# Gates and projections of three branches laid into a sparse attention, and two small moves at the start

## Chip, cores, metric

One core of a Trainium2 chip. The time is that of the device, from the kernel's start to its end, in microseconds (us), as the median of several runs. The profile is of one further execution.

## What is computed

One decoder layer for 512 prompt tokens and 8 sample tokens (each with 2048 cached), all float32, width 1024. The part that matters:

```
h = rms_norm(x, n1);  z = h @ w_in                    # 39 chunks of 128 columns
o_gla, o_hgrn (chunked linear attentions), o_pool (trailing means), o_nsa (sparse attention)
proj = einsum('blnc,ncd->blnd', branches, w_branch)   # 4 x (512 -> 1024)
gate = sigmoid(h @ w_gate + b_gate)                   # 4 x (1024 -> 1024)
x = x + sum_n(gate * proj) @ w_out
u = relu(rms_norm(x, n2) @ w1);  x = x + (u * u) @ w2
fgate = lb + (1 - lb) * sigmoid(hf)                   # lb: from the cumulated softmax of a parameter
```

The sparse attention adds three branches: mean-compressed keys, the 16 best blocks of 64 keys, and a window of 512. For the prompt it is a dense masked attention over up to four blocks of 128 keys; for the samples it reads the caches.

## The kernel before

All 520 tokens are the columns of one stage; activations lie with features on partitions (eight tiles of 128 x 520). A float32 product is made of three fp32r ones: `hi x hi`, `lo x hi`, `hi x lo`. So every weight chunk (128 partitions x 1024, 512 KB) is loaded by SyncE (`load`, `reload`, slots of a ring of four), rounded to its high part by ScalarE (`upper`, L1048) and subtracted for its low part by GpSimd (`lower`, L1876, the operation at L1879). A unit is one chunk times all tokens: `fm_unit` (L545, the matmuls at L555), 48 matmuls of 260 columns into two banks of PSUM. `UNITS_OF` counts the units of each chunk; the semaphores `raw`, `w_hi`, `w_lo` and `prod` chain the four engines. The order on each engine is that in which its block is written.

The stages, in the profiled execution:

- 0 to 50 us: transposes of x, first norm (`norm_apply`, L1303), h in two parts.
- to 437: the 39 chunks of `w_in`, laid between the steps of the two linear attentions, their norms and the pooling. The lower bound's exp is at L1092 (ScalarE), its four small VectorE steps at L1351 to L1354, and TensorE's L616 waits for the VectorE work behind them (`la_ev`, L1357). GpSimd makes the distances of seven levels (L1890, L1891), with low parts between.
- 437 to 509, preparation: norms of the keys, compressed keys of the prompt, masks and small tables. GpSimd gathers the compressed cache of one sample after the other (2 MB each, L1946) into two buffers `Y`, and sums 16 rows to one (L1964, L1965).
- 509 to 657, pair loop: 32 pairs of heads; eight pairs each for one, two, three and four blocks of keys. Each pair: scores (L888), mask and maximum (L1703, L1705), exp (L1219), transposes (L861), copies (L1714), values (L874). The samples' compressed attention and choice of blocks run as single operations between the pairs (`compressed_step`).
- 657 to 736, sample jobs: ten jobs, first two for the window (`Y`, loaded by SyncE), then eight of the chosen cache, each of four slices of 512 KB, gathered by GpSimd (L1980) into a ring `X` of 15. A job: `keys_transposed` (L924), `scores` (L934), `probs_over` (L945), `values` (L955). Its partial sums are merged at L1761 to L1781.
- 736 to 767: x is read back from a spill, h is made again (its place was used by the attention), by `norm_apply`.
- 767 to 1041, mixing: for each of 8 tiles of 128 output columns four gates and four projections: 48 chunks, 64 units. Sigmoid on ScalarE, products and sums on VectorE (`mixT`).
- to 1502: `w_out` with the second norm's sums, the MLP, transposes, output.

## Time and profile before

| | us |
|---|---|
| runs (3): median, lowest, highest | 1506.16, 1505.02, 1507.02 |
| profiled execution, its time | 1503.8 |
| its span, first to last instruction | 1502.0 |
| TensorE busy | 1298.2 |
| VectorE, ScalarE, GpSimd busy | 568.0, 403.9, 542.9 |

The span is what the engines' instructions cover; the time has what lies around it too. A group's mean is the duration of one instruction; TensorE's overlap, so that their rate is the stretch divided by their number. "Idle before" is put down to what released the engine last.

### The profile page before, as it was taken

How to read it: one execution, taken by the hardware profiler on the slowest of the kernel's cores; microseconds unless marked ns; L12 is line 12 of the kernel's file. 1: busy time of each engine (PE TensorE's matmuls, PEld its weight loads, DVE VectorE, ACT ScalarE, POOL GpSimd, SP SyncE). 2: the span in 40 equal slices, each digit the busy share in tenths (PEclk: the TensorE clock that was granted, in tenths of full speed). 3: DMA queues.
4: the chain of work that ended last, by engine and by line, in shares of the span. 5: the costliest groups of instructions: out<-in, count | busy, mean ns of one | idle time of the engine just before them, and what ended most of it. 6: DMA issues, size and time to landing. Idle time of an engine off the chain costs nothing.

```text
span 1502.0 us, 24320 instructions
## 1 busy us (share of the span) xinstructions
PE 1298.2 (86%) x10284; PEld 1220.6 (81%) x10284; DVE 568.0 (38%) x800; ACT 403.9 (27%) x605; POOL 542.9 (36%) x262
## 2 busy tenths in 40 slices
PE   4698998998974477786489999997979999999998
PEld 3598997897863355565389999997969999999998
DVE  3433664261435776764571111112133410134102
ACT  3342212013450123222152322233232211122210
POOL 2335432054129900025033434343324434344341
PEclk9799999999985698898679999999989999999999
DMA  4221001532145510038113232322212322323222
GB/s 160 99 72 56 29 29 57 125 104 79 32 174 218 208 73 1 1 117 332 57 43 99 84 98 84 98 85 83 71 50 91 93 90 85 94 87 96 86 86 83
DMA packets 43585, 139.15 MB, mean 93 GB/s; under 512 B 3975, under 2 KB 15595, under 8 KB 42107
## 3 DMA queue, kind: packets, MB, share of 16 engines
q1 hardware_dynamic: 37762, 104.70, 21.9%
q0 software_dynamic: 5760, 33.56, 6.1%
q8 instruction: 48, 0.79, 0.2%
q14 instruction: 15, 0.11, 0.0%
HBM read 129.97 MB, written 8.49 MB: 92 GB/s over the span
## 4 chain that ended last, share of the span: by engine, by line
PE 76%; DVE 13%; issue 3%; DMA 3%; ACT 2%; POOL 1%; DVEq 0%; ACTq 0%
PE PS L555 53%; PE PS L583 7%; PE PS L635 3%; DVE tmp L1309 2%; DMA M<-cache_slc_kv,idx 2%; PE PS L874 1%; PE PS L888 1%; PE PS L924 1%; DMA M<-weights 1%; DVE hL L1313 1%; DVE M L1714 1%; PE PS L861 1%; PE PS L773 1%; PE PS L726 1%; PE PS L670 1%
## 5 line engine op out<-in xcount | busy, mean ns | idle before, releaser
L1879 POOL TENSOR_TENSOR WL<-M,WH 128x1024 fp32r<-128x1024 f32 x159 | 386.7, 2435 | 693.3 <-ACT WH L1051 693.1
L555 PE MATMUL PS<-hH,WH 128*128 128x260 f32 x1424 | 298.1, 291 | 30.3 <-DVE hL L1313 27.4
L1051 ACT CAST WH<-M 128x1024 fp32r<-128x1024 f32 x159 | 166.2, 1049 | 505.0 <-DMA M<-weights 505.0
L555 PE MATMUL PS<-hL,WH 128*128 128x260 f32 x1424 | 293.2, 288 | 0.0
L555 PE MATMUL PS<-hH,WL 128*128 128x260 f32 x1424 | 292.9, 288 | 0.0
L555 PEld LDWEIGHTS PS<-hH,WH 128*128 128x128 f32 x1424 | 226.2, 194 | 36.6 <-DVE hL L1313 14.0
L555 PEld LDWEIGHTS PS<-hL,WH 128*128 128x128 f32 x1424 | 226.2, 194 | 0.0
L555 PEld LDWEIGHTS PS<-hH,WL 128*128 128x128 f32 x1424 | 226.1, 194 | 0.0
L555 PE MATMUL PS<-uH,WH 128*128 128x260 f32 x512 | 103.2, 283 | 2.4 <-ACT M L1291 2.4
L555 PE MATMUL PS<-uH,WL 128*128 128x260 f32 x512 | 103.2, 283 | 0.0
L555 PE MATMUL PS<-uL,WH 128*128 128x260 f32 x512 | 103.0, 283 | 0.0
L1980 POOL DMA_INDIRECT M<-cache_slc_kv,idx x32 | 30.1, 941 | 163.0 <-DVE M L1727 127.5
L583 PE MATMUL PS<-WH,hH 128*128 128x256 f32 (+1 forms) x280 | 83.9, 300 | 5.2 <-POOL WL L1879 4.3
L555 PEld LDWEIGHTS PS<-uH,WH 128*128 128x128 f32 x512 | 78.9, 188 | 2.8 <-issue 2.8
L583 PE MATMUL PS<-WL,hH 128*128 128x256 f32 (+1 forms) x280 | 79.5, 284 | 0.0
L583 PE MATMUL PS<-WH,hL 128*128 128x256 f32 (+1 forms) x280 | 79.3, 283 | 0.0
L555 PEld LDWEIGHTS PS<-uH,WL 128*128 128x128 f32 x512 | 78.9, 188 | 0.0
L555 PEld LDWEIGHTS PS<-uL,WH 128*128 128x128 f32 x512 | 78.7, 188 | 0.0
L1852 DVE TENSOR_TENSOR tmp<-M 128x520 f32<-128x520 f32 x32 | 38.2, 1192 | 103.8 <-ACT M L1291 103.8
L1862 DVE TENSOR_TENSOR xT<-xT,PS 128x520 f32 x16 | 11.1, 697 | 171.3 <-PE PS L555 171.3
L1964 POOL TENSOR_TENSOR M<-M 128x2048 f32<-128x2048 f32 (+2 forms) x24 | 66.2, 2759 | 7.9 <-DMA M<-cache_cmp_kv,idx 6.6
L1219 ACT ACTIVATE M<-PS,stat 128x128 f32<-128x128 f32 (+3 forms) x64 | 33.2, 523 | 126.7 <-DVE stat L1705 126.7
(347 smaller groups left out, 2008.8 us busy)
## 6 DMA issues: line engine op xcount, KB each, us to landing
M<-weights SPq DMA_DIRECT2D x159, 512.0 KB, 3.5
M<-cache_win_kv SPq DMA_DIRECT2D x2, 2048.0 KB, 7.9
spill<-xT SPq DMA_DIRECT2D x1, 2080.0 KB, 10.2
xT<-spill SPq DMA_DIRECT2D x1, 2080.0 KB, 8.8
M<-x_prompt SPq DMA_DIRECT2D x4, 512.0 KB
y_prompt<-M SPq DMA_DIRECT2D x4, 512.0 KB
con<-tables SPq DMA_DIRECT2D x1, 1437.5 KB, 12.4
M<-state_gla SPq DMA_DIRECT2D x2, 512.0 KB, 6.1
```

What stands on the lines that cost most here:

```text
L555: last = mm(PS[:, bank + h, 0:HALF], w[:, n % 4, k, :], x[:, HALF * h:HALF * h + HALF], start=(start and k == k0 and w is WH and x is hi), ...
L583: last = mm(PS[0:m, bank, 0:pieces * cols], x[:, k, t], w[:, n % 4:n % 4 + pieces, k, 0:cols], start=(k == 0 and x is hH and w is WH), sto ...
L635: last = mm(PS[:, g % 4, 128 * k:128 * k + 128], a, a, start=True, stop=True)
L670: last = mm(o, zt[:, c, head_cols(k, par)[0]], SC[:, 2 * c + par, k], start=True, stop=(c == 0))
L726: last = mm(PS[:, 2 * (e % 2) + h, 0:HALF], ones if kind == "o" else BO, SQ[e % 2][:, HALF * h:HALF * h + HALF], start=True, stop=True)
L1051: nc.scalar.copy(WH[:, n % 4].rearrange("p k n -> p (k n)"), WR[:, n % 4]).then_inc(sem("w_hi"), 1)
L1219: f(P[2 * (p % 2) + c][:, 0:128 * i + 128], PS[:, 2 * (p % 2) + c, 0:128 * i + 128], ACT.Exp, bias=nm[p % 2][:, c:c + 1], accum_out=rs[:, ...
L1309: v.scalar_tensor_tensor(TH[k % 2], xT[:, k], V(g, k, k + 1), RST, ALU.mult, ALU.mult)\
L1852: v.tensor_tensor(US[q % 2], UR[q % 2], UR[q % 2], ALU.mult).then_inc(sem("u_sq"), 1)
L1879: p.tensor_tensor(WL[:, n % 4].rearrange("p k n -> p (k n)"), WR[:, n % 4], WH[:, n % 4].rearrange("p k n -> p (k n)"), ALU.subtract).then ...
L1964: step(p.tensor_tensor(t[:, 0:n], t[:, 0:n], t[:, n:2 * n], ALU.add))
L1980: gp.indirect_dma_start(X[ring(n)].rearrange("p i c -> p (i c)"), None, slices, bass.IndirectOffsetOnAxis(idx[:, at:at + 1], 0)).then_inc( ...
```

## The change

Three of the four branches (pool, gla, hgrn: `ORDER = (2, 0, 1)`) get their gates and projections before the sparse attention is done. Their 36 chunks come first, in three chunks for every 256 output columns (two of gates, one of projections), and are cut into 96 steps `MIX`: a step is half the tokens of one tile of 128 columns, into one bank. A gate step has 24 matmuls, a projection step 12. 32 steps stand in the preparation, 48 in the pair loop (three in two pairs), 16 in the sample jobs. For that:

- h and the weights keep their places through the attention. Weight slots are three while it runs (`slot_of`, `chunk_behind`); the fourth one's high and low parts are buffers `W3` for the compressed cache.
- The compressed cache comes in quarters of a sample: 32 gathers of 512 KB (`CPIECES`), each summed and added up, between the low parts of the chunks. The samples' compressed operations come four half steps later; `SHIFTS` has their places.
- The ring for the sample jobs has ten slices (`XR`), window slices included, and all are issued by GpSimd. Slices 0 to 9 come early: 0 and 1 in the loop, 2 to 5 when the choice of blocks and step 63 are done, 6 to 9 after the loop.
- Banks: the transposed probabilities have one bank (4) instead of two, bank 7 is that of the steps; the jobs' keys have two banks for their transposes instead of four, which VectorE and ScalarE now empty in turn.
- sigmoid(y) is made as tanh(y / 2) + 1, and the sum is halved where `w_out`'s result is added to x. The branch's own high part is `bX`, one buffer for the three.
- The fourth branch remains behind the attention, in 12 chunks and 16 units, with its high and low parts alone; h isn't made again. Its first gate units stand ahead of the merge's transposes. x is read back to another place, `x2`, after the attention.

Apart from that, the lower bound's subtraction goes to VectorE's start, its exp directly behind the first norm's root, its other steps ahead of the gates' copy; the low parts of chunks 9 and 10 go ahead of the first distances. The core of the diff (TensorE's steps also stand at fixed places in the preparation):

```diff
-N_OUT, N_MLP = N_MIX + 48, N_MIX + 56
-UNITS_OF += [1, 1, 2] * 16 + [1] * 72
+N_LAST, N_OUT, N_MLP = N_MIX + 36, N_MIX + 48, N_MIX + 56
+UNITS_OF += [2, 2, 4] * 12 + [1, 1, 2] * 4 + [1] * 72
 NCH = len(UNITS_OF)
+
+
+def slot_of(n):
+
+    return n % 4 if n < N_MIX else n % 3 if n < N_LAST else (n - N_LAST) % 4
+
+
...
+def chunk_behind(n):
+
+    if n < N_MIX or n > N_LAST + 3:
+        return n - 4
+    return n - 3
+
+
+ORDER = (2, 0, 1)
+MIX = []
+for _bi in range(3):
+    for _m in range(4):
+        for _s in range(8):
+            _t = _s // 2 % 2
+            MIX.append((_bi, _m, _t, _s % 2, _s < 4, N_MIX + 12 * _bi + 3 * _m + (_t if _s < 4 else 2)))
...
+PREP, LOOP = 32, 48
+
+
+def mix_bank(k):
+
+    return 7 if PREP <= k < PREP + LOOP else 6 + k % 2
+
+
+def mix_evac(k):
+
+    bi, m, t, h, gate, _ = MIX[k]
+    return ("sg" if gate else "mix_mul"), 16 * bi + 4 * m + 2 * t + h + 1
 
...
-        Y = [R[:, 12416 + 4096 * i:12416 + 4096 * (i + 1)] for i in range(2)]
...
-        X = [R[:, a:a + 1024].rearrange("p (i c) -> p i c", i=4)
-             for a in [7168 + 1024 * i for i in range(5)] + [12416 + 1024 * i for i in range(8)] + [5120, 6144]]
-        AGAIN = list(range(9)) + [13, 14]
...
+        W3 = [R[:, 12416 + 3072:12416 + 4096], R[:, 16512 + 3072:16512 + 4096]]
+        CPIECES = [(x, c) for x in (4, 5, 6, 7, 0, 1, 2, 3) for c in range(4)]
+        SHIFTS = {24: 4, 26: 6, 32: 0, 34: 2}
+        XR = W3 + [zu[:, 0:1024], zu[:, 1024:2048], zg[:, 0:1024], zg[:, 1024:2048]]             + [zt[:, i, CQ:CQ + 1024] for i in range(4)]
...
+            def mix_step(k):
+
+                bi, m, t, h, gate, n = MIX[k]
+                if h == 0 and (gate or t == 0):
+                    pe.wait_ge(sem("w_lo"), n + 1)
+                earlier = [e for e in range(k) if mix_bank(e) == mix_bank(k)]
+                if earlier:
+                    pe.wait_ge(sem(mix_evac(earlier[-1])[0]), mix_evac(earlier[-1])[1])
+                if not gate and t + h == 0 and m == 0:
+                    pe.wait_ge(sem("b_lo"), bi + 1)
+                half = slice(HALF * h, HALF * h + HALF)
+                for c in range(KT if gate else 4):
+                    hi, lo = hk(c) if gate else (bX[:, c], bL[ORDER[bi]][:, c])
+                    at = c if gate else 4 * t + c
+                    for w, x in ((WH, hi), (WH, lo), (WL, hi)):
+                        last = mm(PS[:, mix_bank(k), 0:HALF], w[:, slot_of(n), at, :], x[:, half],
+                                  start=(c == 0 and w is WH and x is hi), stop=(c == (KT if gate else 4) - 1 and w is WL))
+                last.then_inc(sem("prod"), 1)
+
+            def mix_steps(a, b):
+
+                for k in range(a, b):
+                    mix_step(k)
+
...
+                    if p < NP and 3 * p // 2 + c < 3 * (p + 1) // 2:
+                        mix_step(PREP + 3 * p // 2 + c)
...
             def keys_transposed(j):
 
-                b, y, c = JOBS[j]
-                if b:
-                    pe.wait_ge(sem(f"xw{y}"), 16)
-                else:
-                    pe.wait_ge(sem(f"xq{(j - 2) % 4}"), 64 * ((j - 2) // 4 + 1))
+                pe.wait_ge(sem(f"xq{j % 3}"), 64 * (j // 3 + 1))
                 for s in range(4):
-                    if j:
-                        pe.wait_ge(sem(("kx_dve", "kx_act")[s // 2]), 2 * j - 1 + s % 2)
+                    if s >= 2:
+                        pe.wait_ge(sem(("kx_dve", "kx_act")[s % 2]), 2 * j + 1)
+                    elif j:
+                        pe.wait_ge(sem(("kx_dve", "kx_act")[s % 2]), 2 * j)
                     for i in range(4):
-                        last = tr(PS[:, s, 128 * i:128 * i + 128], piece(j, s, i)[0], ident)
+                        last = tr(PS[:, s % 2, 128 * i:128 * i + 128], piece(j, s, i)[0], ident)
                     last.then_inc(sem("ks_mm"), 1)
...
+                    if j < 6:
+                        mix_step(PREP + LOOP + 2 * j + 2)
...
+            act.wait_ge(*done("lb_d"))
+            f(lbv[:, :, 1], lbv[:, :, 0], ACT.Exp).then_inc(once("lb_e"), 1)
...
+            def mix_step(k):
+
+                bi, m, t, h, gate, n = MIX[k]
+                half = slice(HALF * h, HALF * h + HALF)
+                if gate:
+                    act.wait_ge(sem("prod"), units_before(N_MIX) + k + 1)
+                    if bi + m:
+                        act.wait_ge(sem("mix_mul"), 16 * bi + 4 * m - 4 + 2 * t + h + 1)
+                    col = 8 * ORDER[bi] + 2 * m + t
+                    f(SG[t][:, half], PS[:, mix_bank(k), 0:HALF], ACT.Tanh, bias=bgh[:, col:col + 1], scale=0.5)\
+                        .then_inc(sem("sg"), 1)
+                    if m + t == 0 and h == 1:
+                        if bi:
+                            act.wait_ge(sem("prod"), units_before(N_MIX) + 32 * bi)
+                        else:
+                            act.wait_ge(sem("pool_ev"), 4)
+                            act.wait_ge(sem("stored"), 48)
+                        b = ORDER[bi]
+                        nc.scalar.copy(bX, zf[:, 4 * b:4 * b + 4]).then_inc(sem("b_hi"), 1)
+                s = 4 * (not gate) + 2 * t + h
+                if s in (2, 4, 6):
+                    upper(N_MIX + 12 * bi + 3 * m + 1 + s // 2)
+
+            act.wait_ge(sem("st_out"), 128)
...
+                    dve.wait_ge(sem("sg"), u)
+                    if bi > 1 or bi and u > 18:
+                        dve.wait_ge(sem("mix_add"), u - 16 - 2)
+                    out = GP[:, half] if bi else mixT[:, 2 * m + t, half]
+                    v.scalar_tensor_tensor(out, SG[t][:, half], 1.0, PS[:, mix_bank(k), 0:HALF], ALU.add, ALU.mult)\
+                        .then_inc(sem("mix_mul"), 1)
+                    if bi:
+                        dve.wait_ge(sem("mix_mul"), u)
+                        v.tensor_tensor(mixT[:, 2 * m + t, half], mixT[:, 2 * m + t, half], GP[:, half], ALU.add)\
+                            .then_inc(sem("mix_add"), 1)
...
-            norm_apply("n3", "n1")
-            for b in range(4):
-                dve.wait_ge(sem("b_hi"), b + 1)
-                v.tensor_tensor(bL[b], zf[:, 4 * b:4 * b + 4], bH[b], ALU.subtract).then_inc(sem("b_lo"), 1)
-            with dve.Fori(0, 4) as dq:
...
-            for n in range(9):
+            for n in range(11):
                 lower(n)
             gp.wait_ge(sem("cum"), 4)
             distances(0)
-            lower(9)
-            lower(10)
             distances(1)
             for n in (11, 12, 13):
...
+            rows = lambda name: A[name].rearrange("o n (r t) a k d -> (o n r) (t a k d)", t=4)
+
+            def compressed_gather(q):
+
+                if q >= 2:
+                    gp.wait_ge(sem("c_red"), q - 1)
+                x, c = CPIECES[q]
+                gp.indirect_dma_start(W3[q % 2], None, rows("cache_cmp_kv"),
+                                      bass.IndirectOffsetOnAxis(idx[:, NI + NS * c + x:NI + NS * c + x + 1], 0))\
+                  .then_inc(sem(f"xc{q % 2}"), 16)
+
+            def compressed_sum(q):
+
+                x, c = CPIECES[q]
+                gp.wait_ge(sem(f"xc{q % 2}"), 16 * (q // 2 + 1))
+                t = W3[q % 2].rearrange("p (t c) -> p t c", t=4)
+                step(p.tensor_tensor(t[:, 0:2], t[:, 0:2], t[:, 2:4], ALU.add))
+                if c == 0:
+                    if x == 4:
+                        gp.wait_ge(sem("pool_mm"), 4)
+                    if x == 0:
+                        gp.wait_ge(sem("rows_out"), 96)
+                        gp.wait_ge(*done("ckv_mm"))
+                    p.tensor_tensor(S16[x], t[:, 0], t[:, 1], ALU.add).then_inc(sem("c_red"), 1)
+                else:
+                    step(p.tensor_tensor(t[:, 0], t[:, 0], t[:, 1], ALU.add))
+                    gp.wait_ge(sem("c_red"), q)
+                    p.tensor_tensor(S16[x], S16[x], t[:, 0], ALU.add).then_inc(sem("c_red"), 1)
+                if q + 2 < len(CPIECES):
+                    compressed_gather(q + 2)
+
             gp.wait_ge(*done("idx"))
-            gp.wait_ge(sem("prod"), units_before(N_MIX))
-            for x in range(NS + 1):
-                if x < NS:
-                    if x >= 2:
-                        gp.wait_ge(sem("c_red"), x - 1)
-                    gather(Y[x % 2], x, "cache_cmp_kv").then_inc(sem(f"xc{x % 2}"), 16)
-                if x:
-
-                    y = x - 1
-                    gp.wait_ge(sem(f"xc{y % 2}"), 16 * (y // 2 + 1))
-                    if y == 0:
-                        gp.wait_ge(sem("pool_mm"), 4)
-                        gp.wait_ge(sem("stored"), 48)
-                    t = Y[y % 2].rearrange("p (t c) -> p t c", t=16)
-                    for n in (8, 4, 2):
-                        step(p.tensor_tensor(t[:, 0:n], t[:, 0:n], t[:, n:2 * n], ALU.add))
-                    p.tensor_tensor(S16[y], t[:, 0], t[:, 1], ALU.add).then_inc(sem("c_red"), 1)
-
-            gp.wait_ge(sem("on"), 2 * TT)
-            slices = A["cache_slc_kv"].rearrange("o n (r t) a k d -> (o n r) (t a k d)", t=4)
-            for n in range(32):
+            gp.wait_ge(sem("prod"), units_to_free(N_MIX - 4))
+            compressed_gather(0)
+            compressed_gather(1)
+            lower(N_MIX)
+            lower(N_MIX + 1)
+            q = 0
+            for n in range(N_MIX + 2, N_MIX + 22):
+                for _ in range((2, 1, 1)[n % 3] if n < N_MIX + 12 else 3):
+                    if q < len(CPIECES):
+                        compressed_sum(q)
+                        q += 1
+                lower(n)
+
+            def cache_piece(n):
+
+
                 j, s = n // 4, n % 4
-                y, c = JOBS[2 + j][1:3]
-                if 5 <= n < 13:
-                    gp.wait_ge(sem("oq_mm"), 1 + (n - 5) // 4)
-                if n == 13:
-                    gp.wait_ge(sem("ont_mm"), TT)
-                if n >= 15:
-                    before = AGAIN[n - 15] if n < 26 else n - 11
-                    gp.wait_ge(sem("oq_mm"), 3 + before // 4)
-                at = NI + NS + 4 * (4 * y + s) + c
-                gp.indirect_dma_start(X[ring(n)].rearrange("p i c -> p (i c)"), None, slices,
-                                      bass.IndirectOffsetOnAxis(idx[:, at:at + 1], 0)).then_inc(sem(f"xq{j % 4}"), 16)
-            gp.wait_ge(sem("oq_mm"), NJ)
-            with gp.Fori(0, 30) as i:
+                b, y, c = JOBS[j]
+                if n == 0:
+                    gp.wait_ge(sem("c_red"), len(CPIECES))
+                if n == 2:
+                    gp.wait_ge(*done("rank"))
+                if n == 4:
+                    gp.wait_ge(sem("prod"), units_before(N_MIX) + 64)
+                if n == 6:
+                    gp.wait_ge(sem("on"), 2 * TT)
+                if n >= 10 and n % 4 == 2:
+                    gp.wait_ge(sem("oq_mm"), (n - 10) // 4 + 1)
+                x = 4 * y + s
+                if b:
+                    src = A["cache_win_kv"].rearrange("o s (p i) a k d -> p (o s) (i a k d)", i=4)[:, x]
+                    gp.dma_start(XR[n % 10], src).then_inc(sem(f"xq{j % 3}"), 16)
+                else:
+                    at = NI + 4 * NS + 4 * x + c
+                    gp.indirect_dma_start(XR[n % 10], None, rows("cache_slc_kv"),
+                                          bass.IndirectOffsetOnAxis(idx[:, at:at + 1], 0)).then_inc(sem(f"xq{j % 3}"), 16)
+
+            for n in range(2):
+                cache_piece(n)
+            for n in range(N_MIX + 22, N_MIX + 31):
+                lower(n)
+            for n in range(2, 10):
+                cache_piece(n)
+            for n in range(10, 4 * NJ):
+                if n % 4 == 2 and N_MIX + 31 + n // 4 - 2 < N_LAST:
```

## Rows read from the trace of the kernel before

**Rows 1.** The page, parts 1 and 2: share of TensorE, its clock in 40 slices.
```profile
PE 1298.2 (86%) x10284; PEld 1220.6 (81%) x10284; DVE 568.0 (38%) x800; ACT 403.9 (27%) x605; POOL 542.9 (36%) x262
...
PEclk9799999999985698898679999999989999999999
```

**Rows 2.** Busy time by stretch: us, each engine's busy us (instructions), clock, DMA.
```profile
437.00:509.00 72.00, 27.32 (x110) 22.12 (x109) 45.24 (x54) 9.07 (x12) 61.05 (x30) 0.59 0.62 227
509.00:657.00 148.00, 114.82 (x688) 87.18 (x689) 104.78 (x197) 39.52 (x134) 19.73 (x11) 0.84 0.12 43
657.00:736.00 79.00, 54.46 (x620) 42.33 (x622) 35.81 (x55) 20.21 (x49) 30.05 (x32) 0.83 0.66 240
736.00:767.00 31.00, 10.89 (x52) 9.11 (x45) 27.40 (x51) 10.20 (x18) 10.11 (x4) 0.57 0.00 1
767.00:1041.00 274.00, 274.00 (x2267) 274.00 (x2266) 53.93 (x59) 83.36 (x87) 111.38 (x47) 0.99 0.28 90
1041.00:1049.00 8.00, 0.37 (x4) 0.16 (x2) 3.92 (x3) 3.95 (x7) 3.91 (x2) 0.71 0.25 67
```

**Rows 3.** Waits of TensorE, 40 to 440 us: total, times, longest.
```profile
PE PS L616 <- DVE M L1357: 9.5, 1, 9.5
...
PE PS L583 <- POOL WL L1879: 4.3, 1, 4.3
```

**Rows 4.** Timeline of GpSimd, 100 to 130 us: start, us, line, operation.
```profile
106.13 1.90 POOL L1890 TENSOR_TENSOR M<-M 128x1024 f32<-128x1024 f32 x1 [10.80 <-DVE M L1380]
...
109.83 5.73 POOL L1879 TENSOR_TENSOR WL<-M,WH 128x1024 fp32r<-128x1024 f32 x2
```

**Rows 5.** Chain that ended last, 14 to 135 us: start, us, what.
```profile
74.90 13.34 PE PS L555 x96
```

**Rows 6.** Groups of GpSimd by form: count, busy us, mean ns, idle before.
```profile
L1879 POOL TENSOR_TENSOR WL<-M,WH 128x1024 fp32r<-128x1024 f32 x159 | 386.7, 2435 | 693.3 <-ACT WH L1051 693.1
...
L1964 POOL TENSOR_TENSOR M<-M 128x512 f32<-128x512 f32 x8 | 10.4, 1305 | 0.6
...
L1946 POOL DMA_INDIRECT M<-cache_cmp_kv,idx x8 | 7.9, 987 | 20.4 <-PE PS L555 18.5 <-POOL M L1965 1.6 <-issue 0.3
...
L1965 POOL TENSOR_TENSOR M<-M 128x256 f32<-128x256 f32 x8 | 6.7, 834 | 0.6
```

**Rows 7.** The slice gathers' line L1980, to landing.
```profile
DMA to landing us min/median/max: 4.1/5.9/8.7
```

**Rows 8.** Timeline of ScalarE, 430 to 450 us.
```profile
442.59 0.22 ACT L1194 ACTIVATE stat<-stat 128x20 f32<-128x20 f32 x1
```

**Rows 9.** The page, part 6: transfers, issue to landing.
```profile
M<-weights SPq DMA_DIRECT2D x159, 512.0 KB, 3.5
```

**Rows 10.** Timeline of the pair loop, 509 to 657 us.
```profile
520.79 3.81 DVE L1721 TENSOR_TENSOR stat<-stat,M 128x8 f32<-128x8 f32 x1
...
603.55 1.95 PE L831 MATMUL PS<-gaT,M 127*128 127x8 f32 x16 [0.95 <-DVE gaT L1656]
...
646.82 1.13 PE L888 MATMUL PS<-M 64*128 64x512 f32 x4
...
650.59 0.62 PE L861 MATMUL PS<-con,M 128*128 128x128 f32 x4
```

**Rows 11.** Timeline of the sample jobs, 657 to 737 us.
```profile
659.96 1.97 PE L924 MATMUL PS<-con,M 128*128 128x128 f32 x16 [0.18 <-DVE M L1730]
...
725.84 3.68 PE L924 MATMUL PS<-con,M 128*128 128x128 f32 x16 [4.52 <-DMA M<-cache_slc_kv,idx]
...
731.21 1.05 PE L955 MATMUL PS<-M 128*32 128x128 f32 x32
...
735.22 1.08 PE L955 MATMUL PS<-M 128*32 128x128 f32 x32 [0.78 <-DVE M L1795]
```

**Rows 12.** Timeline behind the jobs.
```profile
749.06 0.78 DVE L1808 COPY M<-M 64x16 f32<-64x16 f32 x4
```

**Rows 13.** Timeline of ScalarE in the loop: a table load.
```profile
565.48 1.28 ACT L1205 ACT_TABLE_LOAD   x1
```

More of the change, by code:

```diff
@@ L169, in build @@
         bL = [parts(f"bL{b}", 4 * b * T, 4) for b in range(4)]
-        bH = [parts(f"bH{b}", (16 + 4 * b) * T, 4) for b in range(4)]
-        mL, mH = parts("mL", 32 * T, KT), parts("mH", 16 * T, KT)
+        bX = place("bX", 20 * T, 4 * TM).rearrange("p (i c) -> p i c", c=TM)[:, :, 0:T]
+        bH3 = parts("bH3", ZU * T, 4)
+        mL, mH = parts("mL", 24 * T, KT), parts("mH", 16 * T, KT)
         uH, uL = parts("uH", 0, 16), parts("uL", 16 * T, 16)
@@ L490, in _ @@
                          tail[HIST:HIST + NS]).then_inc(sem("stored"), 16)
-            sp.wait_ge(sem("pd"), 8)
-            sp.dma_start(SPARE, A["spill"]).then_inc(sem("xt_back"), 16)
+            for n in range(N_MIX, N_MIX + 3):
+                reload(n)
             sp.wait_ge(*done("k_norm"))
@@ L974, in _ @@
+            last_gate(0, 1)
             pe.wait_ge(*done("nsa_done"))
[L975 to L989 removed]
@@ L2017 @@
     gate = tiles(a["w_gate"][0]).reshape(4, 8, 128, KT, COLS)
-    branch = [tiles(a["w_branch"][0].reshape(2, 1024, 1024)[i]) for i in range(2)]
-    mix = np.stack([gate[0], gate[1], branch[0], gate[2], gate[3], branch[1]], 1).reshape(48, 128, KT, COLS)
+    branch = [a["w_branch"][0, b].reshape(4, 128, 4, 2, COLS).transpose(2, 1, 3, 0, 4).reshape(4, 128, KT, COLS)
+              for b in range(4)]
+    mix = np.concatenate([np.stack([gate[b, 0::2], gate[b, 1::2], branch[b]], 1).reshape(12, 128, KT, COLS)
+                          for b in (2, 0, 1, 3)])
     w1, w2 = a["mlp_w1"][0], a["mlp_w2"][0]
```

579 lines of the change are left out of this document (326 added, 253 removed).

## The prediction

> **What bounds the kernel now.** I read the page first: TensorE is busy for 86% of the span, and its granted clock dips in one stretch, slices 12 to 20 [rows 1]. The table of stretches shows why [rows 2]. From 767 to 1041 us, the gates and projections of all four branches, 2267 matmuls run in 274 us: 0.121 us each, nothing idle, clock 0.99. From 437 to 767 us, the sparse attention, TensorE issues few instructions, its clock is 0.57 to 0.84, and it waits for VectorE, ScalarE and DMAs in turn. So matmul work of the first kind, put into the holes of the second, is what can be gained. Three quarters of it move: 96 steps, of which 48 gate steps have 24 matmuls (2.90 us) and 48 projection steps 12 (1.45 us), together 209 us. The question is how much the stretches grow when these are laid in. I take the four stages in order, each as growth against the profiled execution.
>
> **Start (to 135 us).** TensorE waits 9.5 us for the gate's VectorE work, and 4.3 us for a low part on GpSimd [rows 3]. The first wait is the lower bound: VectorE waited in its queue for ScalarE's exp of two columns, which stood behind a weight cast and two activations. With exp right after the norm, and its VectorE steps ahead of the gates' copy, nothing of that is left; next in line is a weight chunk that had landed. The second: chunks 9 and 10 (5.73 us on GpSimd) stand between the first two rounds of distances, after the sums that end at 106.1 [rows 4]. They now run ahead of those sums, so chunk 11 comes about 5 us earlier after them. The matmuls behind the first wait began at the lower clock (96 in 13.34 us [rows 5], where 0.121 each would be 11.6), and I assume the same behind the second: 3 us more. The added index operations are six of 128 x 8 or so, beside matmuls already queued. Behind this comes a stretch that is pure TensorE. Total 9.5 + 4.3 + 3: **-17 us** (bounds -8, if the sigmoid chain takes the place, and -20).
>
> **Preparation and pair loop (437 to 657).** The new owner is GpSimd. The cache sums were 8 rounds; now each quarter is gathered by itself: 32 rounds. A round is one addition over 512 elements (1.31), one over 256 and, for three of four, another to accumulate (0.73 to 0.83), a gather (0.99) and some 0.3 of issue: 3.35 or 4.1, mean **3.95 us**; each low part is 2.44 [rows 6]. The order is fixed: 13 rounds and 12 low parts before the 32 preparation steps can end, then three rounds before each of the next six low parts. A gather has two rounds' time less its own additions to land; at 5.9 us [rows 7] that is (5.9 + 3.0) / 2 = 4.45 a round, under which the low parts between fit. Chunk 40 is cast behind the roots of the keys' norms: those end at 442.8 now [rows 8], and get the compressed keys' root with two table loads, some 3 us, and two casts ahead of them, so about 448. From there 13 x 3.95 + 11 x 2.44 + some 5 of first waits = 83 us bring chunk 50 at 532, TensorE's last step at 538. The loop starts at 509 now [rows 2], so preparation grows 29 us for 70 us of matmuls. Weights aren't the limit: 3.5 us from issue to landing [rows 9], against a chunk's 5.8 us of matmuls with two other slots full.
>
> Then 19 rounds and 7 low parts, 92 us: chunk 57 comes at **624**, and pair 11 waits for it. TensorE alone would need some 60 us here; the difference is lost to GpSimd. From pair 11 TensorE is the bound. Its own part of a four-block pair is the distance from scores to the end of the second head: 646.82 to 650.59, 3.8 us [rows 10]; for three and two blocks I scale to 2.7 and 1.9. Each pair gets 1.5 steps, 3.26 us, and I add 0.4 for handovers: 5.6, 6.4 and 7.5 us. 5 x 5.6 + 8 x 6.4 + 8 x 7.5 = 139, the compressed branch's own matmuls 12 (an estimate: six groups like the one of 1.95 us [rows 10]), the last pairs and sums 4: end at **779** against 656.7. Growth **122 us**, with 174 us of matmuls in it (bounds 96, GpSimd hidden, and 165). The score banks are left with one transpose bank less; the copy it waits for (0.7 us) lies under a step, or costs 0.5 where there is one step only.
>
> The rule that speaks against this is the lock. In the trace an 8-column VectorE multiply took 3.81 us at 520.79 [rows 10], while GpSimd was summing the cache. The Trainium skill, "SBUF — State Buffer", section "SBUF: two separate sides", says that a VectorE operation with two SBUF inputs blocks for the whole GpSimd instruction; by it each of the 24 accumulations in the loop could wait up to a low part, which the trace bears out. 24 x 2.44 = 59 us is its upper end; half of a low part each, 29 us, is its price as a rival. In the sum I take it as covered, since VectorE is busy for 105 us of the loop's 148 [rows 2] and the loop gets 122 - 29 = 93 us longer for 24 products and 24 accumulations of 260 columns.
>
> **Sample jobs (657 to 736).** Here I expect a loss. The ring was 15 slices and two window buffers; it is ten, and slices 10 and 11, the second half of job 2, may be gathered only when job 0's values are through. TensorE goes from values(j) straight to the keys of job j + 2, so from job 2 each job waits: 0.3 + 1.25 (second issue) + 5.2 (between 4.1 and 5.9 [rows 7]) = 6.75 us. The 16 steps stand after the first half of the keys and ahead of the values, that is, not under this wait; they push the release back. A job from landed keys to values, 725.84 to 732.3, is 6.4 us at the low clock: the same 16 transposes take 1.97 us warm and 3.68 after 4.5 us of idling for a DMA [rows 11]. Steps add 26 us over eight jobs (five gates, eight projections), and 0.55 a job because the first one starts cold. Period 6.75 + 6.4 + 3.3 + 0.55 = **17.0**; the first values come 21.4 us after the loop (three steps in it), eight periods 136, last values 2.5: 160 us, against 79.6 now (656.7 to 736.3). Growth **80** (bounds 58, warm with landings of 4.1, and 105).
>
> The Trainium skill, "TensorE: Matmul & The Clock Gate", section "What's actually happening", has two levels, 1.2 and 2.4 GHz; 3.68 over 1.97 is near that ratio, and by the level alone all 26 us of steps would be 52 if every job stayed cold. That is the rival on the far side below.
>
> **After the jobs (736 to 1049).** The norm of h again and its splits (749.8 to 767) go; h is kept. nsa_done comes 13.5 us after the last values (749.84 - 736.3 [rows 11, 12]), one gate unit fills it (5.8 us), the second gate unit 5.8 follows, the branch's cast and low part add 4.6 behind nsa_done, so the projections start at 18.5. Then 10 units of 5.8 us: 76.5, and 2 more to the output's first matmul, as the mix's casts are now spread; before, 8 us passed there [rows 2]. 78.5 against 1049.2 - 736.3 = 313: **-234.5**, of which 209 is moved work (bounds -225, if the 2 MB of x2 ahead of chunk 79 bites, and -238). Sigmoid as tanh + 1, halved in the output's addition, replaces one operation by one.
>
> **Sum.** -17 + 122 + 80 - 234.5 = -49.5 on 1503.8 us: 1454.3. The median of the runs is 2.4 above the profiled time, so **1457 us**.
>
> **Rivals.**
> 1. *Jobs better, loop as said*: landings near 4.1 and a warm engine; 8 x 2.6 = 21 less: **1436**. For: a lone gather lands in 4.1. Against: after a wait the transposes ran cold.
> 2. *VectorE's lock becomes the loop's bound*: +29: **1486**. For: 3.81 us for 8 columns; against: VectorE's slack.
> 3. *Rounds cost more*: if gathers compete with weights and rows, a round becomes 4.65: 32 x 0.7 = +22: **1479**.
> 4. *Tanh and exp reload tables.* A change of function cost 1.28 us at 565.48 [rows 13]; two loads for each of 24 gate steps in the loop, half exposed, and 8 later: +35: **1492**. No row shows tanh. (The Trainium skill, "ScalarE: Activation LUTs", section "Table sets: the hidden batching unit", puts both in one set: then nothing.)
> 5. *Slower*: in the jobs the wait keeps TensorE cold throughout. Place: jobs 2 to 9. Price: period 6.75 + 7.1 + 6.6 = 20.4, and with landings at 8.7 [rows 7] 24: 8 x 7 = +56: **1513**. It decides from a period of 23.2 us. For: the clock is 0.83 already, with a wait in only some of the jobs [rows 2]; against: steps are dense work.
> 6. That the steps hide fully, everywhere: under 1424.
>
> **How the numbers follow.** Forecast 0.42 (own range 1443 to 1472); rivals 1 to 6: 0.17, 0.13, 0.09, 0.05, 0.10, 0.04. The range reaches from 1424 to 1494. This kernel's measurement tells 0.2%, 3 us, from nothing. Slower: 0.08 of rival 5 and 0.02 from the tails of 2 and 4; same 0.03; faster 0.87.
>
> **What would show it.** Right: chunk 57's low part near 610 (less 17 for the start), TensorE idle before it; pairs of 7.5 us at the end; job periods of 17 us with a DMA wait near 6 in each; no wait of 9.5 near 65. Wrong: idle TensorE in the late loop (rival 2), table loads beside tanh (4), no DMA wait in the jobs (1), a period over 23 (5).

## The result, and the profile after

| | us | ratio to before, 95% interval |
|---|---|---|
| before, measured beside it (4 runs) | 1506.59 | |
| after (4 runs) | 1530.35, from 1529.07 to 1531.31 | 1.0159, 1.0141 to 1.0176 |
| forecast | 1457, range 1424 to 1494 | |

The change made the kernel 1.6% slower where I forecast 3.3% faster, and the time lies outside my range. TensorE's instructions are as many as before and its share of the longer span is the same 86%. From the page, parts 1 and 2, of the kernel after, beside [rows 1]:

```profile
PE 1310.4 (86%) x10284; PEld 1230.4 (81%) x10284; DVE 573.4 (38%) x823; ACT 394.2 (26%) x615; POOL 587.0 (38%) x350
...
PEclk9899999999987888899997978799989999999999
```

The low clock didn't go: its lowest tenths rose from 5 to 7, over a longer middle. Busy time by stretch of the kernel after (columns as in [rows 2]): preparation, the pairs that GpSimd holds, the late pairs, the sample jobs, the merge, the last branch.

```profile
436.00:541.00 105.00, 86.49 (x578) 83.97 (x577) 37.94 (x54) 21.85 (x30) 72.42 (x58) 0.81 0.38 122
541.00:633.00 92.00, 58.79 (x401) 53.97 (x399) 26.93 (x50) 20.78 (x55) 81.39 (x74) 0.83 0.47 148
648.00:816.00 168.00, 149.00 (x1045) 125.90 (x1044) 98.34 (x159) 48.08 (x114) 31.87 (x17) 0.92 0.14 47
833.00:993.00 160.00, 98.26 (x858) 85.00 (x862) 40.27 (x67) 29.70 (x60) 47.71 (x41) 0.79 0.38 132
993.00:1012.00 19.00, 8.76 (x115) 7.82 (x105) 13.91 (x35) 4.57 (x11) 4.64 (x2) 0.89 0.08 28
1012.00:1077.00 65.00, 65.00 (x534) 65.00 (x534) 24.46 (x27) 21.37 (x26) 24.40 (x10) 0.98 0.35 123
```

The ledger, from the first instruction of each stage in the two traces (the jobs to the end of their last values, at 736.3 and 997.7; `w_out` begins at 1049.2 and 1076.5):

| stage | forecast | measured | off |
|---|---|---|---|
| start, at the last unit of `w_in` (431.61 to 422.26) | -17 | -9.4 | +7.6 |
| preparation and pair loop (end 656.7 to 832.8, less the start) | +122 | +185.5 | +63.5 |
| jobs (79.6 to 164.9) | +80 | +85.3 | +5.3 |
| last values to `w_out` (312.9 to 78.8) | -234.5 | -234.1 | +0.4 |
| sum | -49.5 | +27.3 | +76.8 |

The spans differ by 25.1 (1502.0 to 1527.1); some 2 us are regained behind `w_out`'s first matmul. So one term holds most of the miss, and it has two halves. The forecast had chunk 57's low part done at 624, or 614.6 with the real start: it was done at 638.7, 24.1 late. From there to the end of the loop I gave 155 us: it took 194.1, 39.1 more.

The first half, GpSimd's low parts and the casts that they waited for. From its timeline: start, us, operation, and in brackets the idle time before it. The low parts shown are those of chunks 44, 47, 50 and 57.

```profile
490.58 2.36 POOL L2045 TENSOR_TENSOR WL<-M,WH 128x1024 fp32r<-128x1024 f32 x1 [13.91 <-ACT WH L1138]
...
518.01 2.40 POOL L2045 TENSOR_TENSOR WL<-M,WH 128x1024 fp32r<-128x1024 f32 x1 [4.68 <-ACT WH L1138]
...
544.10 2.36 POOL L2045 TENSOR_TENSOR WL<-M,WH 128x1024 fp32r<-128x1024 f32 x1 [3.28 <-ACT WH L1138]
...
636.08 2.57 POOL L2045 TENSOR_TENSOR WL<-M,WH 128x1024 fp32r<-128x1024 f32 x1
```

And ScalarE's timeline in front of chunk 44's cast: the exponent of the prompt's compressed scores, then the tanh of two steps, then the cast.

```profile
483.95 1.06 ACT L1316 ACTIVATE M<-M 128x1024 f32<-128x1024 f32 x1 [11.06 <-DVE M L1719]
486.20 0.48 ACT L1286 ACTIVATE tmp<-PS,stat 128x260 f32<-128x260 f32 x1 [1.19 <-PE PS L790]
489.08 0.48 ACT L1286 ACTIVATE tmp<-PS,stat 128x260 f32<-128x260 f32 x1 [2.41 <-PE PS L790]
489.46 1.04 ACT L1138 CAST WH<-M 128x1024 fp32r<-128x1024 f32 x1
```

GpSimd stood 13.9 us at this one low part, with 27 rounds of the compressed cache behind it in its queue that needed nothing from ScalarE. With chunk 41's 4.6 the waits are 26.5 us, and the low part of chunk 40, where they begin to count, was itself done at 442.7, 4 us behind the forecast (448, less the start's 9.4). The rounds themselves went as forecast: 92.2 us from the end of chunk 50's low part (546.5) to that of chunk 57's, where 92 were said.

The second half. Maxima of pairs 11 and 31 before, then after (timelines of VectorE):

```profile
540.19 0.69 DVE L1705 TENSOR_REDUCE stat<-PS 128x2 f32<-128x512 f32 x1
...
648.46 1.23 DVE L1705 TENSOR_REDUCE stat<-PS 128x2 f32<-128x1024 f32 x1
```

```profile
647.72 0.69 DVE L1863 TENSOR_REDUCE stat<-PS 128x2 f32<-128x512 f32 x1
...
816.20 1.23 DVE L1863 TENSOR_REDUCE stat<-PS 128x2 f32<-128x1024 f32 x1
```

These 20 pairs took 108.3 us before and take 168.5 now. Busy time of that stretch before, and of the steps' matmuls alone in the one after:

```profile
540.00:648.50 108.50, 86.71 (x515) 64.64 (x514) 75.18 (x134) 28.55 (x86) 0.00 (x0) 0.87 0.00 1
```

```profile
648.00:816.00 168.00, 75.70 (x549) 70.27 (x547) 0.92 0.14 47
```

TensorE was busy for 80% of these pairs before, 21.8 us idle in 108.5. The steps bring 75.7 us, the stretch grows by 60, and 19.0 us are still idle. So the steps found next to no holes: the idle time fell by 2.8 us. The other 13 us between 75.7 and 60 are TensorE's busy time outside the steps, 73.3 us (149.0 - 75.7) where it was 86.7. Not all of that is faster work. Records of neighbouring matmuls overlap, and a moment in which both a step and a pair are busy counts among the steps; the pairs' values, transposes and scores, each line for itself, take 78.9 us where they took 83.2.

The jobs did what the forecast said. TensorE between two jobs' values in the kernel after (the steps' own lines left out):

```profile
898.06 1.97 PE L987 MATMUL PS<-con,M 128*128 128x128 f32 x8 [7.00 <-DMA M<-cache_slc_kv,idx]
...
902.28 1.04 PE L987 MATMUL PS<-con,M 128*128 128x128 f32 x8
903.15 0.60 PE L1010 MATMUL PS<-con,M 128*128 128x128 f32 x4
904.04 1.07 PE L999 MATMUL PS<-M 128*32 128x512 f32 x8 [0.29 <-DVE M L1904]
...
908.11 1.08 PE L1020 MATMUL PS<-M 128*32 128x128 f32 x32
```

A wait of 7.0 us here and of 7.2 in the mean of eight, the longest 9.5 (6.75 forecast), first keys cold at 1.97 for 8 (1.04 for the second 8), a mean period of 17.2 us (17.0 forecast). Everything between the keys and the values is covered, and the steps stand there, while the wait behind the values has nothing in it.

### The profile page after: what moved, and what is told of

Read it like the earlier page. It is cut to its first block, busy times and chain, and to the rows that moved or that the text cites. A ratio compares the mean times of both kernels' runs of the same rounds, so it can differ in the third digit from the quotient of the medians.

```text
span 1527.1 us, 24112 instructions
## 1 busy us (share of the span) xinstructions
PE 1310.4 (86%) x10284; PEld 1230.4 (81%) x10284; DVE 573.4 (38%) x823; ACT 394.2 (26%) x615; POOL 587.0 (38%) x350
## 3 DMA queue, kind: packets, MB, share of 16 engines
q1 hardware_dynamic: 36706, 100.50, 20.1%
## 4 chain that ended last, share of the span: by engine, by line
PE 71%; DVE 9%; POOL 9%; DMA 3%; ACT 3%; issue 3%; DVEq 0%; POOLq 0%; ACTq 0%
PE PS L582 38%; PE PS L790 10%; PE PS L610 7%; DMA M<-cache_slc_kv,idx 3%; PE PS L662 3%; POOL WL L2045 2%; POOL M L2125 2%; PE PS L987 2%; POOL M L2116 1%; PE PS L922 1%; PE PS L935 1%; PE PS L951 1%; DVE tmp L1431 1%; POOL M L2134 1%; POOL M L2136 1%
## 5 line engine op out<-in xcount | busy, mean ns | idle before, releaser
L582 PE MATMUL PS<-hH,WH 128*128 128x260 f32 x1040 | 218.1, 292 | 22.2 <-DVE hL L1435 18.8
L582 PE MATMUL PS<-hL,WH 128*128 128x260 f32 x1040 | 213.9, 288 | 0.0
L582 PE MATMUL PS<-hH,WL 128*128 128x260 f32 x1040 | 213.8, 288 | 0.0
L582 PEld LDWEIGHTS PS<-hH,WH 128*128 128x128 f32 x1040 | 165.3, 194 | 27.5 <-issue 11.4
L582 PEld LDWEIGHTS PS<-hL,WH 128*128 128x128 f32 x1040 | 165.2, 194 | 0.0
L582 PEld LDWEIGHTS PS<-hH,WL 128*128 128x128 f32 x1040 | 165.0, 194 | 0.0
L790 PE MATMUL PS<-hH,WH 128*128 128x260 f32 x384 | 124.3, 324 | 36.0 <-POOL WL L2045 35.8
L790 PE MATMUL PS<-hL,WH 128*128 128x260 f32 x384 | 119.1, 310 | 0.0
L790 PE MATMUL PS<-hH,WL 128*128 128x260 f32 x384 | 118.5, 309 | 0.0
L790 PEld LDWEIGHTS PS<-hH,WH 128*128 128x128 f32 x384 | 84.5, 220 | 41.1 <-POOL WL L2045 37.7
L790 PEld LDWEIGHTS PS<-hL,WH 128*128 128x128 f32 x384 | 84.1, 219 | 0.0
L790 PEld LDWEIGHTS PS<-hH,WL 128*128 128x128 f32 x384 | 83.4, 217 | 0.0
L582 PEld LDWEIGHTS PS<-uH,WH 128*128 128x128 f32 x512 | 78.9, 188 | 2.8 <-issue 2.8
L2017 DVE TENSOR_TENSOR tmp<-M 128x520 f32<-128x520 f32 x32 | 42.5, 1329 | 100.0 <-ACT M L1413 100.0
L987 PE MATMUL PS<-con,M 128*128 128x128 f32 x160 | 29.1, 342 | 58.4 <-DMA M<-cache_slc_kv,idx 57.3
```

Of the source, the lines that this page charges most:

```text
L582: last = mm(PS[:, bank + h, 0:HALF], w[:, slot_of(n), k, :], x[:, HALF * h:HALF * h + HALF], start=(start and k == k0 and w is WH and x is ...
L790: last = mm(PS[:, mix_bank(k), 0:HALF], w[:, slot_of(n), at, :], x[:, half], start=(c == 0 and w is WH and x is hi), stop=(c == (KT if gat ...
L987: last = tr(PS[:, s % 2, 128 * i:128 * i + 128], piece(j, s, i)[0], ident)
L2017: v.tensor_tensor(US[q % 2], UR[q % 2], UR[q % 2], ALU.mult).then_inc(sem("u_sq"), 1)
```

## Experiments

My theories after the comparison: GpSimd's fixed order, with the casts it waits for, holds preparation and first pairs; in the jobs the steps stand in the wrong place; the late pairs are set either by VectorE's handovers, one transpose bank among them, or by TensorE's own work.

**1. The start alone**, on the kernel before (the diff is the last hunks of the change: exp and subtraction moved, `range(9)` to `range(11)`).

> The kernel before with the two small moves alone: the lower bound's operations ahead of the matmuls and the low parts of chunks 9 and 10 ahead of the distances. My theory (the moves take away one wait of TensorE and pull the low parts of 11 to 13 forward, as the changed kernel's trace shows, where the last unit of w_in ends 9.4 us earlier): 1497 us, between 1494 and 1500, faster by 0.5 to 0.8%. Rival (the 9.4 us are given back by the time of the pair loop or the jobs, whose transfers and low parts keep their own pace): 1503 to 1507.

1494.02 us, ratio 0.9923 (0.9905 to 0.9940): 11 us where it isn't followed by the rest, against 17 forecast.

**2. The bound's part of it alone**, the low parts of 9 and 10 left behind the first distances.

> The kernel before with the lower bound's operations moved alone; the two low parts stay behind the first distances. My forecast priced the bound's part at 9.5 us and the low parts at 4.3 and 3; both together measured about 11 us. Theory (the bound's wait is the larger part): 1498 to 1503 where both together gave 1494. Rival (the low parts alone gave it): 1503 to 1507.

1495.89 us, 0.9925 (0.9907 to 0.9943): the same ratio, so the times don't show the low parts' share. The bound's move is nearly all. First matmul behind the distances, before its 135.7, here and then with both moves (line, instruction, durations, first and last start):

```profile
L637 PE MATMUL PS<-M x64: 272/272/373, 127.2 to 135.4; 64*128 64x128 f32 x64
```

```profile
L637 PE MATMUL PS<-M x64: 272/272/373, 124.3 to 132.5; 64*128 64x128 f32 x64
```

8.5 us from the bound, 2.9 from the low parts, which I had priced at 4.3 + 3. The wait that I priced didn't go, and nor did the low clock behind it: TensorE still stands at chunk 11's low part, for 4.31 us with the bound's move alone and for 4.14 with both, only 3.4 us earlier, and from 110 to 115 us the granted clock is 0.50 with both. Its wait, with the bound's move alone and then with both:

```profile
PE PS L583 <- POOL WL L1881: 4.3, 1, 4.3
```

```profile
PE PS L583 <- POOL WL L1881: 4.1, 1, 4.1
```

One reason: the sums that the distances wait for now run beside the two low parts that were moved. VectorE's four sums after and before:

```profile
91.41 8.43 DVE L1505 TENSOR_TENSOR_SCAN M<-con,M 128x512 f32<-128x512 f32 x4
```

```profile
101.49 4.56 DVE L1380 TENSOR_TENSOR_SCAN M<-con,M 128x512 f32<-128x512 f32 x4
```

8.43 us for what took 4.56. The two experiments differ alike: 8.43 with both moves, where the longest of the four takes 3.35 us, and 4.56 with the bound's alone, the longest 1.22. The Trainium skill, "SBUF — State Buffer", section "SBUF: two separate sides", has a VectorE operation with two SBUF inputs and a GpSimd operation that reads SBUF wait for each other, the later one for the whole of the earlier; the trace agrees, with 3.9 us lost beside low parts of 2.4 and 2.7 us.

**3. Both steps of a job behind its values**, on the kernel after:

```diff
                     last.then_inc(sem("ks_mm"), 1)
-                    if s == 1:
-                        mix_step(PREP + LOOP + j + min(max(j - 1, 0), 6))
...
                     scores(j + 1)
-                    if j < 6:
-                        mix_step(PREP + LOOP + 2 * j + 2)
                 values(j)
+                if j < 8:
+                    mix_step(PREP + LOOP + 2 * j)
+                    mix_step(PREP + LOOP + 2 * j + 1)
```

(likewise on ScalarE and VectorE; GpSimd's low parts 71 to 74 go behind the first four gathers that a job releases.)

> The changed kernel with both steps of a sample job put right behind the job's values and ahead of the next keys, where TensorE waits about 7 us for the gather (57.3 us in 8 waits). Theory (the wait is a fixed time from the values, about 7 us, so two steps of together 4 to 5.5 us in it are free): the waits fall to about 2 us each, the handovers that the steps covered come back at 0.5 to 1.5 us a job, jobs 160 -> 128 to 138 us, total 1500 to 1508. Rival A (the copies and the exponent behind the keys need the steps' cover as much): jobs 150 us or more, total 1518 to 1530. Rival B (the gathers are late for their own reason and move with the queue): no change, 1527 to 1533.

1496.84 us, 0.9942 (0.9923 to 0.9961), 34 us less than after and better than I expected. Waits for the gathers, total, times, longest (57.3 in 8 before the edit):

```profile
PE PS L987 <- DMA M<-cache_slc_kv,idx: 19.6, 8, 4.9
```

The mean period is 12.65 us instead of 17.2, the whole stage 123.5 instead of 164.9. That is 41 us; 4 of them are lost ahead of the jobs, where nothing was edited: pair 11's maximum stands at 652.0 in this trace, at 647.7 in that of after. The handovers needed no cover worth naming. So the wait was in my forecast, to half a microsecond, and what stood in the wrong place cost more than the whole change was slower by.

**4. The rounds thinned**, on the kernel after: additions of 8 elements instead of 512 and 256 (the sums are left out, so the kernel only serves to read the path).

> The changed kernel with its 32 rounds of the compressed cache thinned: the gathers stay, the three additions of a round are cut to 8 elements a row (their sums are left out, so this time is only for reading the path). Theory (GpSimd, in order, bounds the preparation and the first pairs): a round falls from 4.15 to about 1.9 us, chunk 57's low part comes about 40 us earlier or more, the pair loop ends 30 to 50 us earlier, total 1480 to 1500. Rival (TensorE and VectorE's handover take over at once, since the late pairs cost as much as the early): total 1515 to 1528.

1482.06 us. Chunk 57's low part is done 47 us earlier, at 591.5, the loop ends at 781.8 (51 earlier), and the late part between them takes 190.3 us where it took 194.1. GpSimd bounds the first half and has next to nothing to do with the second.

**5. The casts one step earlier**, the additions whole:

```diff
-                if s in (2, 4, 6):
-                    upper(N_MIX + 12 * bi + 3 * m + 1 + s // 2)
+                if s in (1, 3, 5):
+                    upper(N_MIX + 12 * bi + 3 * m + 1 + (s + 1) // 2)
```

> The changed kernel with ScalarE's casts of the mix chunks one step earlier (behind the first, third and fifth step's place instead of the second, fourth and sixth). Theory (GpSimd stood 4.6, 13.9, 4.7 and 3.3 us at low parts whose cast was not done, with its rounds queued behind them, and the early loop is bound by GpSimd): chunk 50's low part 15 to 25 us earlier, total 1508 to 1518. Rival (casts wait for the weights' transfer, so ScalarE is held instead and its exponents with it): 1528 to 1540.

1508.89 us, 1.0020 (1.0001 to 1.0039): 21 us less than after from two lines, as the theory said. Low parts of chunks 44, 50 and 57 (490.58, 544.10 and 636.08 before the edit):

```profile
479.77 2.39 POOL L2045 TENSOR_TENSOR WL<-M,WH 128x1024 fp32r<-128x1024 f32 x1 [8.80 <-ACT WH L1138]
...
525.40 2.40 POOL L2045 TENSOR_TENSOR WL<-M,WH 128x1024 fp32r<-128x1024 f32 x1
...
616.99 2.35 POOL L2045 TENSOR_TENSOR WL<-M,WH 128x1024 fp32r<-128x1024 f32 x1
```

The late part is 190.3 us, as in experiment 4 and 3.8 less than in the changed kernel. Most of the first half of the miss, 19 of 24 us, is this.

**6. One transpose bank in the kernel before**, `PS[:, (4, 7)[c]` to `PS[:, 4` with the wait for the last copy.

> The kernel before with the transposes of both heads of a pair in one PSUM bank, as the changed kernel has them (its second bank went to the steps). Theory (part of the 39 us that the late pairs cost above my forecast is this handover: a head's transposes now wait until VectorE has copied the other's): the pair loop 8 to 25 us longer, 1513 to 1530. Rival (the loop's matmuls and the exponent hide it, as the waits of only 0.3 to 2.4 us each suggest): 1503 to 1509.

1531.38 us, 1.0160 (1.0143 to 1.0178): the lost bank alone costs the kernel before 23.5 us, its pair loop 25.4. Its maxima of pairs 11 and 31 stand at 548.1 and 672.0: 123.9 us for the 20 pairs, where 108.3 were. TensorE's largest wait from 540 to 672 us, the late pairs:

```profile
PE PS L861 <- DVE M L1714: 21.9, 20, 2.7
```

I had priced that bank at 0.5 us where one step covers it.

**7. The second head's transposes in its own score bank**, on the kernel after:

```diff
-                    last = tr(PS[:, 4, 128 * j:128 * j + 128], P[...
+                bank = 2 * (p % 2) + 1 if c else 4
+                    last = tr(PS[:, bank, 128 * j:128 * j + 128], P[...
...
+                        if p >= 2 and c:
+                            pe.wait_ge(sem("pt_ev"), 2 * p - 2)
```

> The changed kernel with the second head's transposes in that head's own score bank (free once its exponent is taken), so that the two heads of a pair no longer share one bank. Theory (the shared bank cost the kernel before 23.5 us and its pair loop 25.4 us, and the late pairs of the changed kernel are set by such handovers, since cutting the steps' matmuls shortened them by only 28 us of 197): the late stretch 197 -> 175 to 185 us, the loop's start unchanged (GpSimd), total 1508 to 1520. Rival (with steps between the two heads' transposes the copy is covered already, 9.6 us in 8 waits is all there is): 1522 to 1531.

1529.88 us, 1.0145 (1.0126 to 1.0165): no difference that can be told from after. The waits of L922 on VectorE are gone from the late pairs, whose 20 periods fall from 168.5 to 162.5 us, but pair 11 came 5 us later. Experiment 3's trace has its pair 11 as late (652.0), with the shared bank and 168.6 us behind it. The rival was right: with steps between the heads' transposes the copy is covered. What cost 23.5 us in the kernel before costs at most 6 here. Why pair 11 was later in the two traces isn't settled.

**8. The loop's steps thinned** to 3 matmuls each, on the kernel after (their sums are left out, again only to read the path):

> The changed kernel with the 48 steps of the pair loop cut to their first product chunk (3 matmuls each instead of 24 or 12; their sums are left out, so this time is only for reading the path); waits, tanh, products and low parts stay. Theory (from chunk 57 on TensorE's own matmuls are most of the loop, 175.7 us busy in 200, and before it GpSimd is the bound): the stretch from chunk 57's low part to the transposes behind the loop 197 -> 130 to 150 us, the stretch before it unchanged within 10 us, total 1465 to 1485. Rival (VectorE's order sets the late pairs): it stays above 165 us, total 1490 or more.

1507.13 us. The late part falls by 27 us (from 194.1 to 166.9), so my expectation was wrong, and both numbers are where the rival had them: 54.7 us of the steps' busy time were taken out between pairs 11 and 31, and half of that came off. Whole stretch from pair 11 to 31, and the steps' part of it:

```profile
651.00:792.00 141.00, 103.23 (x588) 76.94 (x588) 99.70 (x161) 46.99 (x114) 31.37 (x17) 0.85 0.17 51
```

```profile
651.00:792.00 141.00, 21.00 (x90) 15.01 (x90) 0.85 0.17 51
```

The other half came back in two ways. TensorE's idle time is 38 us instead of 19: with the matmuls cut, the copies that they covered stand free, 19.7 of it waiting for L1873's copies in 17 places (6.9 in 5 before the cut). And its busy time without the steps is 82.2 us at a granted clock of 0.85, against 73.3 (149.0 - 75.7) with full steps at 0.92. Part of these 9 us is again the overlap of records; values, transposes and scores, each line for itself, go from 78.9 to 86.4 us, and the lower clock is what I put that down to. No run changes the clock alone.

So this experiment doesn't decide between TensorE's own work and VectorE's handovers as the bound of the late pairs. The 20 pairs took 123.9 us with one bank and no steps (experiment 6), 141 with the thin steps' 21.0 us and 168.5 with the full ones' 75.7. The first 21 us of steps hid 4 of themselves, the next 54.7 hid 27. I read it so: full steps fill the path and cover waits at once, and the sum of the pairs' own work and the steps' is what holds. That reading is argued from these sums.

**9. Casts earlier, and ten low parts on VectorE** (chunks 41 to 50), GpSimd doing 22 rounds in one go, then 2 before each low part:

```diff
+                if s in (2, 4, 6) and n_low < V_LOW:
+                    dve.wait_ge(sem("w_hi"), n_low + 1)
+                    dve.wait_ge(sem("w_lo"), n_low)
...
-                for _ in range((2, 1, 1)[n % 3] if n < N_MIX + 12 else 3):
+                for _ in range(22 if n == V_LOW else 2):
```

> The changed kernel with the casts one step earlier, as in the last study, and the low parts of the first branch's chunks 41 to 50 on VectorE, so that GpSimd does 22 rounds without a stop, then two in front of each low part. Theory (GpSimd in its order was the bound of the preparation and the first pairs, and late pairs have their own pace of 193 us): chunk 57's low part at 585 to 600 instead of 617 there and 636 in the changed kernel, loop end at 780 to 795, total 1478 to 1492. Rival (VectorE, 2 us a low part under GpSimd's lock, holds the preparation instead): 1500 or more.

1492.40 us, 0.9894 (0.9860 to 0.9927). Right in direction, short in size: chunk 57's low part begins at 603.1 and the loop ends at 798.6. The time is 16.5 us under experiment 5's.

**10. The same with experiment 3.**

> The last kernel and the steps behind the values together. Theory (the two stretches are separate, gains add): 1530 - 35 (jobs) - 22 (casts) - 15 to 25 (low parts) = 1448 to 1462, faster than both kernels. Rival (the earlier loop end lets the jobs meet transfers or a cold TensorE): 1470 or more.

1450.47 us, 0.9621 (0.9595 to 0.9647): faster than both kernels, 3.8% under before. The gains of the two stretches add, 33.5 and 38.0 us apart and 79.9 together; the 8 us above the sum are not explained. The 20 late pairs take 158.2 us here. The page of this kernel:

```profile
PE 1291.7 (89%) x10284; PEld 1209.9 (83%) x10284; DVE 585.3 (40%) x833; ACT 394.0 (27%) x615; POOL 571.2 (39%) x340
...
PEclk8799999999998998999998989899989999999999
```

**11. Its rounds spread** as 18, 3, 3, 3, 3, 2.

> The kernel of 1450 us with the rounds spread as 18, 3, 3, 3, 3, 2 and the shared bank left. Theory (TensorE's 14.9 us wait for chunk 51 goes, some comes back as waits for the next low parts): 1440 to 1447. Rival (the 32 rounds are the bound to their end wherever they stand): 1447 to 1454.

1450.34 us, 0.9622 (0.9604 to 0.9639): nothing. Low parts of chunks 51 and 57, with 22 rounds first and then with 18 (both wait for a cast at chunk 57, the rounds being done):

```profile
546.69 2.35 POOL L2050 TENSOR_TENSOR WL<-M,WH 128x1024 fp32r<-128x1024 f32 x1
...
604.74 2.36 POOL L2050 TENSOR_TENSOR WL<-M,WH 128x1024 fp32r<-128x1024 f32 x1 [3.91 <-ACT WH L1138]
```

```profile
532.53 2.40 POOL L2050 TENSOR_TENSOR WL<-M,WH 128x1024 fp32r<-128x1024 f32 x1 [2.62 <-ACT WH L1138]
...
604.94 2.36 POOL L2050 TENSOR_TENSOR WL<-M,WH 128x1024 fp32r<-128x1024 f32 x1 [2.42 <-ACT WH L1138]
```

14 us earlier at chunk 51, nothing at chunk 57. The rounds are a fixed amount that GpSimd has to be through with before chunk 56 (598.5 and 600.1) wherever they stand. Chunk 57 then waits for its cast in both, so the pair doesn't say which of the two holds the late pairs. TensorE's waits for low parts from 541 us on are 20.1 us in the one and 18.9 in the other.

**12. With the own bank of experiment 7.**

> The fastest kernel so far (1450) with the second head's transposes in their own bank and GpSimd's rounds spread as 18, then 3, 3, 3, 3, 2 in front of a low part, where it had 22 and TensorE waited 14.9 us for chunk 51. Theory (both stretches are on the path): 1450 - 10 to 20 (bank) - 5 to 10 (spread) = 1422 to 1436. Rival (bank hidden by steps, rounds only moved): 1442 to 1452.

1454.04 us (1444.22 to 1456.16), 0.9650 (0.9631 to 0.9668): not faster. The 20 late pairs take 156.6 us, against 158.1 with the shared bank (experiment 11); the bank is no lever once steps lie between.

## Why the prediction was wrong, by its steps

- **Start, -17: short by 7.6.** The bound's 9.5 held (8.5 in experiment 2). The 4.3 and the 3 for a cold TensorE gave 2.9 together, for neither went: the changed kernel still waits 4.1 us for that low part, and its clock still falls behind it. In the changed kernel the gain is 12.4 at 231.7 us and 9.4 at the end of `w_in`. The 3 us between went in a stretch that I had called pure TensorE, to a lower granted clock in two groups: 96 matmuls took 14.36 us at 0.80 (before 13.03 at 0.89), and 48 took 7.51 at 0.77 (before 5.97 at 1.00). Why the clock was lower there isn't known; experiment 1 has 6.01 us for the second.
- **Chunk 50's low part at 532: failed, 24 us** (546.5, where 522.6 was due). Round and low part were priced rightly (4.15 where I had 4.1 for a round with its accumulation, 2.4 where I had 2.44). "Some 5 of first waits" was the error: they were 26.5. I followed GpSimd's own operations and the gathers' landing, but not the casts: a cast has its place in ScalarE's order behind a step's tanh, for chunk 44 behind the compressed scores' exponent too, which waits for VectorE. Experiment 5 moved only the casts, and chunk 57 came 19 us earlier.
- **"From pair 11 TensorE is the bound": near, it is busy for 149 of 168 us. 5.6, 6.4 and 7.5 us a pair: failed, 39 us with the loop's ends.** Twenty periods took 168.5 us where the terms give 145: busy time outside the steps, that is the pairs' own work and the compressed matmuls, is 73.3 (I had 72), the steps' 540 matmuls 75.7 (65, at 0.121 each; they ran at 0.14), idle 19 (8). The other 16 us are at the ends: 9.0 from chunk 57's low part to pair 11's maximum and 16.6 from pair 31's to the end, where the sum had 10. The error of method: 145 against the 108.3 of before lets 28 us of the steps vanish. Of these, 14 are idle time, which I took at 8 us where the trace of before has 21.8, in waits of 0.7 to 4.8 us; it hardly fell. The other 15 are the pairs' own work taken at 72 us where the trace of before has TensorE busy for 86.7; that came out near by count, partly for the overlap of records, and I hadn't seen that I was counting on it. Four of the 39 us went with the earlier casts (experiment 5); what sets the rest of the late pairs' pace, TensorE's sum alone or VectorE's handovers with it, stays open (experiment 8).
- **The transpose bank at 0.5 us: right in place, its size in part by luck.** It is cheap because steps cover it (experiments 6 and 7), as I had said. But I had put a copy left uncovered at 0.5 to 0.7 us, and the same edit without steps costs 23.5 over the loop.
- **Jobs, +80: right** (85.3), with the wait, the cold keys and the period as worked out.
- **After the jobs, -234.5: right** (-234.1).
- **Rivals.** 2, the lock, has its mark in the scans and not in the loop: the 32 accumulations take 0.429 us in the median, the longest 3.16, and TensorE's whole idle time in the late pairs is 19 us. 3: rounds 4.15, not 4.65. 4: no table load beside any tanh. The Trainium skill, "ScalarE: Activation LUTs", section "Table sets: the hidden batching unit", puts tanh and exp in one set, and the trace agrees: none of the 48 tanh has a load, and the loop's only two loads, at 707.8 and 709.4, belong to the samples' ln and the exp behind it. 5, the slower case, had the right sign and the wrong mechanism: the period was 17.2, not 23. The case that came true, several waits on a third engine and late pairs at their full sum, wasn't among them.

## What to carry to other kernels

When work is laid into another stage, price each stretch as the sum of both works on the bound engine, and subtract at most the idle time that the trace shows there. Here that gives 108.3 + 65 - 21.8 = 152 us for the late pairs, a lower bound: it was 168.5, since the steps ran slower and the idle time stayed. An engine that works in order and serves the filler is followed through every wait of its producers too: here a cast in ScalarE's order held back rounds that needed nothing from it. Filler belongs straight in front of the wait that it is to cover: the same 16 steps, moved by half a job (with the places of four low parts), were worth 34 us.

## What the runs showed of the hardware that I had not expected

- Four scans of 512 columns on VectorE take 8.43 us beside GpSimd's subtractions of 1024 columns (experiment 1), and 4.56 without (experiment 2).
- With matmuls taken away the others took longer: from 1045 instructions in 168 us to 588 in 141 us the granted clock went from 0.92 to 0.85, and the pairs' values, transposes and scores from 78.9 to 86.4 us.
